# A hybrid decoder step on one core: work moved to ScalarE, softmax heads started ahead of v's rows, and a crossed first down pair

## What is computed

```
n = rms_norm(x);  p = n @ w_in -> q, k, v, qi, ki, wi, u
indexer: I[t,s] = sum_h wi[t,h] * relu(qi[t,h] . ki[s])          16 heads of 64
attention: softmax over the top 128 (prompt) or 256 (sampled) keys by I, 8 heads, 2 KV heads of 128
group B: g = a * sigmoid(gate);  y = causal depthwise conv of g, width 31, + bias
         y = silu(layer_norm(y))                                  1024 channels
h = x + concat(attention, y) @ w_out
h = h + (silu(n2 @ w_gate) * (n2 @ w_up)) @ w_down;  out = rms_norm(h)      n2 = rms_norm(h), d_ff 5632
```

## Time and profile before

| | us |
|---|---|
| median of 3 runs | 2555.69 (2552.79 to 2559.7) |
| the profiled execution, its own time | 2557.96 |
| its span | 2556.3 |
| TensorE busy / weight load busy | 2478.4 / 2399.4 |
| VectorE / ScalarE / GpSimd busy | 1200.3 / 831.6 / 401.7 |

### The profile page before, as it was taken

The page is one execution under the profiler, slowest core; times in us unless marked ns, Lnnn a source line. Parts: engine busy times, 40 slices in busy tenths (PEclk is TensorE's granted clock), DMA queues, the critical chain, the costliest instruction groups (busy, mean ns, idle before and its releaser), DMA issues.

```text
span 2556.3 us, 49900 instructions
## 1 busy us (share of the span) xinstructions
PE 2478.4 (97%) x19410; PEld 2399.4 (94%) x19412; DVE 1200.3 (47%) x1786; ACT 831.6 (33%) x1076; POOL 401.7 (16%) x438
## 2 busy tenths in 40 slices
PE   6999999998989999999999999999999999999998
PEld 6967999897669999999999999999999999999998
DVE  5588989996433343333333333333333333233354
ACT  6154444224432243333223333223333222222233
POOL 2324899653430000000000000000000000000000
PEclk9999999999999999999999999999999999999999
DMA  7414232214684343232233322233232233322222
GB/s 243 113 31 119 74 84 81 79 51 150 211 255 115 104 112 97 84 90 66 85 104 91 90 83 77 79 92 104 82 90 82 71 88 104 90 86 87 68 86 97
DMA packets 424726, 255.04 MB, mean 100 GB/s; under 512 B 19979, under 2 KB 413443, under 8 KB 423968
## 3 DMA queue, kind: packets, MB, share of 16 engines
q1 hardware_dynamic: 412864, 224.91, 30.4%
q0 software_dynamic: 11792, 29.23, 3.5%
HBM read 243.66 MB, written 11.27 MB: 100 GB/s over the span
## 4 chain that ended last, share of the span: by engine, by line
PE 82%; DVE 5%; issue 4%; POOL 4%; ACT 2%; DMA 1%; SPq 0%; DVEq 0%; POOLq 0%; ACTq 0%
PE ps L1507 76%; POOL y L563 3%; PE ps L1767 1%; PE ps L1600 1%; PE ps L1741 1%; PE ps L1723 1%; DVE ps L1139 1%; PE ps L1787 1%; DMA xN<-in_x_prompt 1%; ACT tap L739 1%; POOL wlo L553 0%; DMA stN<-in_state_conv 0%; POOL y L601 0%; DVE y L1292 0%; PE ps L1731 0%
## 5 line engine op out<-in xcount | busy, mean ns | idle before, releaser
L948 DVE TENSOR_TENSOR wlo<-raw,whi 128x1024 fp32r<-128x1024 f32 (+1 forms) x358 | 437.5, 1223 | 1117.8 <-ACT whi L624 1105.2
L1507 PE MATMUL ps<-xhi,whi 128*128 128x272 f32 (+1 forms) x4512 | 939.8, 290 | 19.7 <-POOL wlo L553 5.7
L1507 PE MATMUL ps<-xhi,wlo 128*128 128x272 f32 (+1 forms) x4512 | 937.4, 289 | 0.0
L1507 PE MATMUL ps<-xlo,whi 128*128 128x272 f32 (+1 forms) x4512 | 934.0, 289 | 0.0
L624 ACT CAST whi<-raw 128x1024 fp32r<-128x1024 f32 (+1 forms) x410 | 428.9, 1047 | 1202.5 <-PE ps L1507 1128.1
L1507 PEld LDWEIGHTS ps<-xhi,whi 128*128 128x128 f32 (+1 forms) x4512 | 712.2, 189 | 23.6 <-issue 11.1
L1507 PEld LDWEIGHTS ps<-xlo,whi 128*128 128x128 f32 (+1 forms) x4512 | 712.1, 189 | 0.0
L1507 PEld LDWEIGHTS ps<-xhi,wlo 128*128 128x128 f32 (+1 forms) x4512 | 707.1, 189 | 0.0
L1507 PE MATMUL ps<-hidh,whi 128*128 128x272 f32 x1408 | 291.2, 288 | 4.6 <-DVE hidl L1446 4.6
L1507 PE MATMUL ps<-hidl,whi 128*128 128x272 f32 x1408 | 290.7, 287 | 0.0
L1507 PE MATMUL ps<-hidh,wlo 128*128 128x272 f32 x1408 | 290.6, 287 | 0.0
(11 more groups left out here) (303 smaller groups left out, 1575.9 us busy)
## 6 DMA issues: line engine op xcount, KB each, us to landing
raw<-in_w_gate SPq DMA_DIRECT2D x88, 512.0 KB, 3.8
raw<-in_w_up SPq DMA_DIRECT2D x88, 512.0 KB, 3.8
raw<-in_w_in SPq DMA_DIRECT2D x72, 512.0 KB, 3.8
raw<-in_w_down SPq DMA_DIRECT2D x64, 384.0 KB, 3.3
raw<-in_w_down SPq DMA_DIRECT2D x64, 320.0 KB, 3.1
raw<-in_w_out SPq DMA_DIRECT2D x32, 512.0 KB, 5.2
ring_pages<-in_cache_k SPq DMA_DIRECT2D x40, 128.0 KB, 3.4
ring_pages<-in_cache_k POOLq DMA_DIRECT2D x40, 128.0 KB, 2.4
```

Of the source, the lines that this page charges most:

```text
L948: ve.tensor_tensor(wlo[:, u.slot, :, 0:cols], raw[:, u.slot, :, 0:cols], whi[:, u.slot, :, 0:cols].bitcast(F32), ALU.subtract).then_inc(s_ ...
L1507: ins = te.matmul(ps[0:cols, 2 * slot + half, 0:HALF], w[:, u.slot, t, 0:cols], x[:, k0 + t, HALF * half:HALF * half + HALF], start=(hf == ...
```

## The change

1. ScalarE copies the 80 rows of the first tile out of PSUM (`kiraw`); VectorE works from that copy, and scales the index tables first, the others after.
2. ScalarE makes `qiS` within its loop of relus, at n = 30 (`s_qi` replaces one count of `s_wtc`); VectorE makes `wsel` ahead of a low part; TensorE turns batch 1's index pages before it waits for the queries; GpSimd's load of the state waits on `s_qi`.
3. ScalarE adds the bias to the sampled part of y, eight activations, ahead of its next weight casts (`s_sbias`).
4. The 32 heads begin before v's rows are turned: x = 0 and 1 use banks 0 and 1 (the banks of all heads are renumbered, not shown), v's rows follow at x = 2. A dummy exponential loads the table early. The splits of y are made one per head, at x = 2 to 9 on ScalarE and x = 3 to 10 on VectorE. `qpad` is filled earlier.
5. The first down pair of each chunk is written out with its units crossed: both slots' first halves, then both second halves; loads and VectorE's wait follow that order.

```diff
                 load(Unit(p0 + j, q), col((w_gate, w_up)[q // 2], P * CJ * c + P * j, q % 2))
-        with sp.Fori(0, 8) as i:
+        for q in range(4):
+            hf = q // 2
+            load(Unit(p0 + CJ, q), w_down[:, bass.ds(CJ * c + DK[0] * hf, DK[hf]), P * (q % 2):P * (q % 2) + P],
+                 k=DK[hf])
+        with sp.Fori(1, 8) as i:
...
     pool.wait_ge(s_is, 3 * IH)
-    pool.wait_ge(s_wtc, 2)
+    pool.wait_ge(s_qi, 1)
...
         hi(Unit(-1, 2 + q))
+    act.wait_ge(s_mm, 3)
+    nc.scalar.copy(halves(kiraw[:, :]), acc(1, 0, 80)).then_inc(s_ev, 1)
...
         nc.scalar.activation(relI[n // 2 % 2][:, n % 2, 0:SW[i]], ps[:, 4 + n % 4, 0:SW[i]], ACT.Relu).then_inc(s_ir, 1)
+        if n == 30:
+            act.wait_ge(s_proj, 9)
+            act.wait_ge(s_pool, 5)
+            for half in range(2):
+                for src in range(2):
+                    last = nc.scalar.copy(
+                        qiS[64 * half:64 * half + 64, :, half, src::2, :].rearrange("p b j t -> p j b t"),
+                        qT[64 * src:64 * src + 64, :, SEQ:NT].rearrange("p j (b t) -> p j b t", t=T))
+            last.then_inc(s_qi, 1)
...
     state_rows(CT - 1)
+    act.wait_ge(s_ssum, CT)
+    for c in range(CT):
+        last = nc.scalar.activation(y[:, c, SEQ:NT], y[:, c, SEQ:NT], ACT.Identity, bias=vec[:, 32 + c:33 + c])
+    last.then_inc(s_sbias, 1)
...
     act.wait_ge(s_ysl, CT)
-    act.wait_ge(s_mm, 2 * M_OUT)
-    for c in range(CT):
-        nc.scalar.copy(xhi[:, 8 + c, :], y[:, c, :]).then_inc(s_yh, 1)
-        if c == 1:
-            act.wait_ge(s_nt, 3)
-            rows_out(nc.scalar, vN, flat[:, 2048:3072], ps[0:NS, 6, 0:256], 256, s_nc)
...
+    nc.scalar.activation(stat[:, 62:63], stat[:, 0:1], ACT.Exp)
...
                 act.wait_ge(s_pt, x - 2)
-            nc.scalar.activation(pP[:, x % 3, 0:w], ps[:, (4, 5, 0, 1)[x % 4], 0:w], ACT.Exp,
+            nc.scalar.activation(pP[:, x % 3, 0:w], ps[:, (0, 1, 4, 5)[x % 4], 0:w], ACT.Exp,
...
+        if x == 1:
+            act.wait_ge(s_nt, 3)
+            rows_out(nc.scalar, vN, flat[:, 2048:3072], ps[0:NS, 6, 0:256], 256, s_nc)
+        if 0 <= x - 2 < CT:
+            c = x - 2
+            act.wait_ge(s_mm, 2 * M_OUT)
+            nc.scalar.copy(xhi[:, 8 + c, :], y[:, c, :]).then_inc(s_yh, 1)
...
-            nc.scalar.copy(pPT[:, z % 2, 0:nb, :], ps[:, (6, 2)[z % 2], 0:P * nb].rearrange(
+            nc.scalar.copy(pPT[:, z % 2, 0:nb, :], ps[:, (2, 6)[z % 2], 0:P * nb].rearrange(
...
     dve.wait_ge(s_cc, 3)
-    ch.link(ve.tensor_tensor(tab[:, :, :], tab[:, :, :], rstd1[:, :].unsqueeze(1).to_broadcast([P, 4, NT]),
+    ch.link(ve.tensor_tensor(tab[:, 2:4, :], tab[:, 2:4, :], rstd1[:, :].unsqueeze(1).to_broadcast([P, 2, NT]),
...
-    dve.wait_ge(s_mm, 3)
-    ki2 = halves(kiT[:, :])
-    ve.tensor_tensor(ki2[0:64], acc(1, 0, 64), c2[0:64], ALU.mult)
-    ve.tensor_tensor(rt2[0:32], acc(1, 32, 64), s2[0:32], ALU.mult)
-    ve.tensor_tensor(rt2[32:64], acc(1, 0, 32), s2[32:64], ALU.mult)
-    ve.tensor_tensor(halves(wT[:, :]), acc(1, 64, 80), rs2[0:16], ALU.mult).then_inc(s_ev, 1)
...
+    ve.tensor_tensor(kiT[0:64, :], kiraw[0:64, :], tab[0:64, 2, :], ALU.mult)
+    ve.tensor_tensor(rt[0:32, :], kiraw[32:64, :], tab[0:32, 3, :], ALU.mult)
+    ve.tensor_tensor(rt[32:64, :], kiraw[0:32, :], tab[32:64, 3, :], ALU.mult)
+    ch.link(ve.tensor_tensor(wT[:, :], kiraw[64:80, :], rstd1[0:16, :], ALU.mult))
...
+    ch.link(ve.tensor_tensor(tab[:, 0:2, :], tab[:, 0:2, :], rstd1[:, :].unsqueeze(1).to_broadcast([P, 2, NT]),
+                             ALU.mult))
...
         ve.tensor_tensor(dst, dst, rt2, ALU.add).then_inc(s_proj, 1)
-    def pair(p, first, second, mid=None, lows=True, last_low=True):
+    def pair(p, first, second, mid=None, lows=True, last_low=True, crossed=0):
...
-        dve.wait_ge(s_mm, 4 * p + 4)
+        dve.wait_ge(s_mm, 4 * p + 4 + crossed)
...
                                     ALU.mult, ALU.add).then_inc(s_ia, 1)
-    lo(Unit(P_QI + 3, 7))
-    dve.wait_ge(s_proj, 9)
...
-    for half in range(2):
-        for src in range(2):
-            last = ve.tensor_copy(qiS[64 * half:64 * half + 64, :, half, src::2, :].rearrange("p b j t -> p j b t"),
-                           qT[64 * src:64 * src + 64, :, SEQ:NT].rearrange("p j (b t) -> p j b t", t=T))
...
-    last.then_inc(s_wtc, 1)
...
     last.then_inc(s_wtc, 1)
+    lo(Unit(P_QI + 3, 7))
...
     convolved(CT - 1)
-    dve.wait_ge(s_ssum, CT)
-    ve.tensor_tensor(y[:, :, SEQ:NT], y[:, :, SEQ:NT], vec[:, 32:40].unsqueeze(2).to_broadcast([P, CT, NS]),
-                     ALU.add).then_inc(s_ssum, 1)
...
     block_counts()
-    pair(P_V, lambda: plain(tile_of(vT, 0), 0), lambda: plain(tile_of(vT, 1), 1), mid=choose, lows=False)
-    for c in range(CT):
-        dve.wait_ge(s_yh, c + 1)
-        ve.tensor_tensor(xlo[:, 8 + c, :], y[:, c, :], xhi[:, 8 + c, :].bitcast(F32), ALU.subtract
-                         ).then_inc(s_mix, 1)
...
-    for kv in range(NKV):
-        last = ve.tensor_copy(
-            qpad[:, :, kv, 16 * kv:16 * kv + 16].rearrange("p b (g t) -> p g b t", g=GRP),
-            qT[:, GRP * kv:GRP * kv + GRP, SEQ:NT].rearrange("p g (b t) -> p g b t", b=B))
-    last.then_inc(s_qp, 1)
...
+    def padded_queries():
...
+        for kv in range(NKV):
+            last = ve.tensor_copy(
+                qpad[:, :, kv, 16 * kv:16 * kv + 16].rearrange("p b (g t) -> p g b t", g=GRP),
+                qT[:, GRP * kv:GRP * kv + GRP, SEQ:NT].rearrange("p g (b t) -> p g b t", b=B))
+        last.then_inc(s_qp, 1)
...
+    def choose_and_pad():
...
+        choose()
+        padded_queries()
...
+    pair(P_V, lambda: plain(tile_of(vT, 0), 0), lambda: plain(tile_of(vT, 1), 1), mid=choose_and_pad, lows=False)
...
                              stat[:, 28 + z % 4:29 + z % 4], None, ALU.mult).then_inc(s_pn, 1)
+        if 0 <= x - 3 < CT:
+            c = x - 3
+            dve.wait_ge(s_yh, c + 1)
+            ve.tensor_tensor(xlo[:, 8 + c, :], y[:, c, :], xhi[:, 8 + c, :].bitcast(F32), ALU.subtract
+                             ).then_inc(s_mix, 1)
...
         if not last:
-            with dve.Fori(0, 8) as i:
+            pair(p0 + CJ, lambda: add(0, 0), lambda: add(1, 1), crossed=1)
+            with dve.Fori(1, 8) as i:
...
-            with dve.Fori(0, 7) as i:
+            pair(p0 + CJ, lambda: final(0, 0), lambda: final(1, 1), crossed=1)
+            with dve.Fori(1, 7) as i:
...
                       ).then_inc(s_hs, 1)
+    for g in range(2):
+        turn(1, g)
...
-    pe.wait_ge(s_wtc, 2)
+    pe.wait_ge(s_qi, 1)
...
-            if b < B - 1:
+            if 0 < b < B - 1:
...
-            pe.wait_ge(s_wtc, 3)
+            pe.wait_ge(s_wtc, 2)
...
     pe.wait_ge(s_conv, CN * CT)
-    pe.wait_ge(s_ssum, CT + 1)
+    pe.wait_ge(s_sbias, 1)
...
     tile(P_V, 1)
-    pe.wait_ge(s_ev, M_OUT)
-    pe.wait_ge(s_nc, 2)
-    in_rows(vT)
...
-    pe.wait_ge(s_nc, 3)
+    pe.wait_ge(s_ev, M_OUT - 1)
...
+        if x == 2:
+            pe.wait_ge(s_ev, M_OUT)
+            pe.wait_ge(s_nc, 2)
+            in_rows(vT)
+            pe.wait_ge(s_nc, 3)
...
-            bank = (4, 5, 0, 1)[x % 4]
+            bank = (0, 1, 4, 5)[x % 4]
...
             pair(p0 + j)
-        with pe.Fori(0, 8) as i:
+        for hf in range(2):
+            pe.wait_ge(s_hid, CJ * c + (DK[0] if hf == 0 else CJ))
+            for s in range(2):
+                if hf == 0:
+                    pe.wait_ge(s_ev, 2 * (p0 + CJ) + s)
+                unit(Unit(p0 + CJ, 2 * hf + s), s, hf, k=DK[hf], k0=DK[0] * hf, xh=hidh, xl=hidl)
+        with pe.Fori(1, 8) as i:
```

More of the change, by code:

```diff
@@ L195, in build @@
         rt = at("rt", [P, NT], F32, R0 + 23936)
+        kiraw = at("kiraw", [80, NT], F32, R0 + 16384)
         gbuf = at("gbuf", [P, SEQ + CK - 1 + B * (CK - 1 + T)], F32, R0)
@@ L264, in build @@
         s_it, s_ic = sem("s_it"), sem("s_ic")
+        s_qi, s_sbias = sem("s_qi"), sem("s_sbias")
         s_dt, s_dr, s_hs, s_xs = sem("s_dt"), sem("s_dr"), sem("s_hs"), sem("s_xs")
@@ L1348, in _ @@
                         dve.wait_ge(s_p, x - 3)
[L1349 removed]
+                    ve.reduce_max(stat[:, 36 + x % 4:37 + x % 4], ps[:, (0, 1, 4, 5)[x % 4], 0:w], AX.X
                                   ).then_inc(s_nm2, 1)
```

3 lines of the change are left out of this document (1 added, 2 removed).

## The result

The changed kernel takes 2535.01 us, median of 4 runs (2531.74 to 2541.45), against 2554.61 us for the kernel before in the same session: ratio 0.9923, 95% interval 0.9898 to 0.9948. It is faster by 19.6 us; the forecast was 2528.6 with a range of 2520 to 2540. The profiled execution took 2531.74 us (span 2530.1), so the two profiled spans differ by 26.2, and the medians by 6.6 less. Both differences have to be explained, and they have different causes. The forecast is 6.4 too low, and the measured median lies nearer to the 2533 and 2536 of the rivals than to it; the median can't tell which mechanism held, the traces can.

What follows compares the result with a forecast made beforehand. TensorE, busy 97% of the span, was taken as the bound, so only its waits and slow-clock time could be won: 6.5 + 4.5 + 7.5 + 4.0 + 4.6 = 27.1, from 2557.96 to 2530.9, median 2528.6, range 2520 to 2540.

Steps and rivals of the forecast that it cites:

- first tile: At the first tile, TensorE's 3.70 us wait and the half-clock stretch behind it go: 6.5 us won.
- index stage: Up to the state turn: earlier state load, landing in 9 us at 205.0, less 0.1 stall: 4.5 us won.
- behind the convolution: From bias add to pair of k: VectorE wins 9.8, loses 2.3 beside low parts; k begins 7.5 us earlier.
- softmax heads: Start of the heads: first turn 6.9 us sooner, splits in eight rounds cost some back: 4.0 net.
- first down pairs: In four chunks, the 1.15 us wait for hidl is covered by crossed half units: 4.6 us won.
- 0 to 0.6 of stall; I take 0.1: Index head loop: four ScalarE query copies, covered by 1.35 us of buffers, stall VectorE's loop by 0.1 us.
- 7.0 x (1 - 0.58) = 2.9 behind it: Index stage, TensorE's path: the slow-clock stretch behind the 3.0 us wait for queries goes too, 2.9 us.
- Page numbers late: Index stage rival: GpSimd's 32 reads end near 180, wins only 2.25; 7.5 us less, 2536; chance 0.12.
- VectorE held at the port: Rival behind the convolution: first top-k copy held as long as the bias add, VectorE's gain lost, 2536; chance 0.10.
- Transfer and splits exposed: Rival: state load takes 11.3 again, head splits hide nothing; 2.3 + 2.3 us less, 2533; chance 0.17.
- Slower through the heads' clock: Rival in the heads: waits in split rounds drop TensorE's clock to 1.2 GHz, up to 53 us added, 2582; chance 0.03.
- the median of the runs lies 2.3 below that execution: Final step: forecast execution of 2530.9 us becomes a median of 2528.6 by the 2.3 gap of the kernel before.

Runs made afterwards that it cites:

- i_pages_warm: Changed kernel with spread query copies, late-batch pages split 4 GpSimd and 12 SP, three unused matmuls at the head loop's end; 2538.41 us.
- i_vector: Changed kernel with the four query copies back on VectorE behind the head sums, batch 1's turns still ahead; 2533.78 us, ratio to before 0.9918.
- i_spread: Changed kernel with ScalarE's four query copies one each behind heads 12, 16, 20 and 24; 2532.43 us, ratio to before 0.9913.
- best: Changed kernel with spread copies, unused matmuls, 6/10 pages, GpSimd's first low part of k's pair earlier, k's first tile read between sorts; 2522.37 us.
- u_bias: Changed kernel with the sampled bias add back on VectorE; 2538.57 us, ratio to before 0.9929.
- low1: Changed kernel with GpSimd's first low part of the pair of k ahead of its eight products; 2535.63 us, ratio to before 0.9917.
- i_spread_state: Changed kernel with spread query copies and the state's load issued behind the late pages of two of four batches; 2537.98 us, ratio 0.9927.

## Why the prediction was right or wrong

The median fell inside the range. Of the five terms the index stage's failed, the last one was 1.1 too small, and so failed the step from the traces to the medians.

The terms, in us. "The two traces" is the changed kernel's stage against the stage before; the index change as a whole was not undone.

| term | forecast | the two traces | undone |
|---|---|---|---|
| first tile | 6.5 | 6.5 | 6.6 |
| index stage | 4.5 | 1.4 | |
| behind the convolution | 7.5 | 7.3 | 6.6 |
| softmax heads | 4.0 | 4.3 | 4.1 |
| first down pairs | 4.6 | 5.7 | 5.7 |

**First tile, convolution, heads** came out with their mechanisms. The copy took 0.61 against the bound of 1.05. VectorE's loss beside the low parts, taken as 2.3 between 0 and 4.3, was 3.5: the pair of k moved by 14.9 where 8.6 lay ahead of it, so VectorE won 6.3 of the 9.8. That the term still came to 7.3 is 1.0 of half clock saved behind the pair of k, which I had declined to count: two misses that cancel, and so luck. The first rounds with a split in the heads are 1.42, not 1.66, and the turn came at 3.8, not 4.1. In the trace 0.75 of the earlier index start came from an input that landed sooner, not from the change.

**First down pairs** was mis-sized: I priced the wait and not the restart behind it, 0.27 each time.

**Index stage** is where the prediction failed. Its sum went by the path of the state's load, and two steps of that path were mis-sized. The first is the stall, "0 to 0.6 of stall; I take 0.1", from "3 x 0.61 - 0.49 = 1.35 us of cover": four copies of 0.40 cost the head loop 0.6 in four of seven traces (28.56 against 27.94), and 1.5 in the other three, the profiled one among them, where the clock fell behind the stall. The second is "so I take 9": the load took 10.8. Counted from the first index turn, the load was issued 53.4 later, before 54.3, so 0.8 earlier instead of 2.2, and it landed 0.5 sooner instead of 2.3. Together that is the 1.4 of the table.

TensorE's own path failed as well, at the step "7.0 x (1 - 0.58) = 2.9 behind it", which let the slow stretch go with the wait. The wait went; the stretch stayed, in every one of twelve traces that have no unused matmuls at the loop's end (both with them have none). It hangs on the 1.0 to 1.2 that TensorE stands at the loop's end (i_pages_warm fills that wait and changes nothing else), which I had not looked at. So the turn forecast for 177.1 came at 180.66, and the 203.5 at which TensorE was to be ready, 1.5 ahead of the load, was as much too early. The two paths ended together. With the stall gone the state turn still came late: in i_vector 63.5 behind the first index turn, with the state landed at 62.4, where the forecast was 205.0 - 144.0 = 61.0. The last pages end there too (i_spread waits 2.48 for them). Neither the spread copies nor the earlier load with them shortened the stage (63.81 and 63.83); best, which moved all of the paths, did.

The Trainium skill ("VectorE: DVE Perf Modes", the TRN2 errata) was right on the copies: its 224 + N cycles are an estimated 0.40 each, and the trace has 0.392 to 0.405. The stall was larger than the 0.25 worked out from it.

**Rivals.** Page numbers late: no, GpSimd goes on at once behind the last head sum (174.43). VectorE held at the port: no, the first two top-k copies beside the low parts took 1.07 and 1.48. The rule of the Trainium skill ("GPSIMD Engine Reference", Key points) does show, in the bias add (9.81 in u_bias) and in the sort steps of low1. Transfer and splits exposed: in part, the load at 10.8 and splits that cost 2.9 in all, so they hid 2.3, as taken. Slower through the heads' clock: not as priced, though the clock does fall there in some executions (below).

**From traces to medians.** The terms add to 27.1 and the traces differ by 26.2, but the medians by 19.6. The failed step is "the median of the runs lies 2.3 below that execution", carried over to the changed kernel. The kernel before's profiled execution lay 3.3 above the median of its session, and the changed kernel's happened to be its fastest, 3.3 below its median; that is the 6.6. Of the forecast's miss of 6.4, 0.9 lies in the trace (2531.74 against 2530.9) and the rest here. What makes an execution slow can be read from the table: up to 6.8 in the start (141.1 to 147.9), 3.3 in the FFN, up to 1.3 in the heads, up to 1.7 in the index stage. The changed kernel's profiled execution had the best pace in the FFN and the heads, and a start 2.2 above the best. Executions of the kernel before in these sessions ran from 2549.60 to 2561.46. The start varies with the landing of the first weights: ScalarE, which also casts x, stood 4.3 us for them in i_spread_state's start (147.9) and not at all in best's (141.1). That the unprofiled runs vary for the same reasons is likely but not shown.

## What to carry to other kernels

A slow-clock stretch need not belong to the longest wait near it: here it stayed when the wait of 3.0 went. Before counting it as won, look for a shorter stop ahead of it that might cause it just as well, and if there is one, fill it and see. When several paths end within a microsecond or two of each other, shortening one shows nothing: list each path's end before pricing a move. Compare edits stage by stage between marks of the code, since untouched stages of this kernel differ by up to 7 us between executions.
